# Post-norm weights moved into ScalarE's copy of the output group; the residual scaled and added two chunks at a time

## The reference, cut to what matters

```python
def rms_norm(x, g):
    xf = x.astype(jnp.float32)
    y = xf * lax.rsqrt(jnp.mean(xf * xf, axis=-1, keepdims=True) + EPS)
    return (y * g.astype(jnp.float32)).astype(x.dtype)

def half_ffn(x, g_pre, g_post, w_in, w_out):
    gate, up = jnp.split(rms_norm(x, g_pre) @ w_in, 2, axis=-1)
    return x + 0.5 * rms_norm((jax.nn.silu(gate) * up) @ w_out, g_post)
...
    for i in range(DEPTH):
        xp = half_ffn(xp, g[0], g[1], ffn_w_in[i, 0], ffn_w_out[i, 0])
        ...
        xp = xp + rms_norm(yp, g[3])
        ...
        xp = half_ffn(xp, g[4], g[5], ffn_w_in[i, 1], ffn_w_out[i, 1])
```

## Time and profile before

| | |
|---|---|
| time, median of 3 runs | 2374.84 us (2372.28 to 2375.91) |
| span of the profiled execution | 2375.1 us |
| PE busy | 2213.7 us, 93% of the span |
| DVE busy | 1457.4 us, 61% |
| ACT busy | 941.8 us, 40% |
| POOL busy | 158.0 us, 7% |
| granted TensorE clock, mean | 0.955 of full speed |

### The profile page before, as it was taken

How to read it: one execution, slowest core, us unless ns; L and a number is a source line. 1 busy time by engine, 2 the same in 40 slices (tenths; PEclk the granted TensorE clock), 3 DMA queues, 4 the chain that set the end, 5 groups by cost and what they waited for, 6 DMA issues and landing times.

```text
span 2375.1 us, 41971 instructions
## 1 busy us (share of the span) xinstructions
PE 2213.7 (93%) x17475; PEld 2129.9 (90%) x17475; DVE 1457.4 (61%) x1727; ACT 941.8 (40%) x1111; POOL 158.0 (7%) x214
## 2 busy tenths in 40 slices
PE   7999989999999979899999999779999999998997
PEld 6999989998998945789989998468999999898997
DVE  5665866646655567366656645655664665686663
ACT  3443344444434335244344434324443444433442
POOL 3001010001001000010010001001000000101000
PEclk9999999999999989889999999979999999898998
DMA  6554445553554434245545554414554555354550
GB/s 204 177 196 142 160 144 163 185 201 125 177 195 136 161 113 142 89 142 178 188 131 178 186 188 141 143 45 127 183 189 149 166 185 187 118 178 133 185 188 28
DMA packets 286121, 370.76 MB, mean 156 GB/s; under 512 B 12247, under 2 KB 212360, under 8 KB 285924
## 3 DMA queue, kind: packets, MB, share of 16 engines
q1 hardware_dynamic: 282378, 364.57, 46.0%
q10 hardware_dynamic: 3610, 4.28, 0.5%
HBM read 364.87 MB, written 8.11 MB: 157 GB/s over the span
## 4 chain that ended last, share of the span: by engine, by line
PE 56%; DVE 5%; POOL 1%; issue 1%; ACT 0%; ACTq 0%; DVEq 0%; POOLq 0%
PE ps L1371 15%; PE ps L1373 15%; PE ps L1372 15%; PE ps L1423 1%; PE ps L1424 1%; PE ps L1427 1%; PE ps L1677 1%; POOL rs L609 1%; PE ps L1590 1%; DVE kt_dec L1176 1%; DVE probs L1123 1%; PE ps L1547 1%; PE ps L1580 1%; PE ps L1379 1%; PE ps L1390 1%
## 5 line engine op out<-in xcount | busy, mean ns | idle before, releaser
L1371 PE MATMUL ps<-x_hi,w_high_ring 128*128 128x264 f32 x3112 | 893.8, 287 | 0.0
L860 DVE TENSOR_TENSOR w_low_ring<-wstage,w_high_ring 128x2048 fp32r<-128x2048 f32 x332 | 728.4, 2228 | 262.7 <-ACT w_high_ring L630 184.2
L1373 PE MATMUL ps<-x_hi,w_low_ring 128*128 128x264 f32 x3112 | 889.2, 286 | 0.0
L1372 PE MATMUL ps<-x_lo,w_high_ring 128*128 128x264 f32 x3112 | 888.2, 285 | 0.0
L1372 PEld LDWEIGHTS ps<-x_lo,w_high_ring 128*128 128x128 f32 x3112 | 592.8, 190 | 0.0
L1371 PEld LDWEIGHTS ps<-x_hi,w_high_ring 128*128 128x128 f32 x3112 | 591.3, 190 | 0.8 <-issue 0.2
L1373 PEld LDWEIGHTS ps<-x_hi,w_low_ring 128*128 128x128 f32 x3112 | 591.5, 190 | 0.0
L1371 PE MATMUL ps<-h_hi,w_high_ring 128*128 128x264 f32 x1664 | 474.4, 285 | 4.1 <-issue 4.1
L1373 PE MATMUL ps<-h_hi,w_low_ring 128*128 128x264 f32 x1664 | 474.9, 285 | 0.0
L1372 PE MATMUL ps<-h_lo,w_high_ring 128*128 128x264 f32 x1664 | 473.2, 284 | 0.0
L630 ACT ACTIVATE w_high_ring<-wstage 128x2048 fp32r<-128x2048 f32 (+2 forms) x172 | 307.1, 1816 | 311.6 <-PE ps L1373 299.7
(11 more groups left out here) (287 smaller groups left out, 1898.5 us busy)
## 6 DMA issues: line engine op xcount, KB each, us to landing
wstage<-in_ffn_w_in_dram SPq DMA_DIRECT2D x352, 512.0 KB, 5.0
wstage<-in_ffn_w_out_dram SPq DMA_DIRECT2D x160, 512.0 KB, 4.6
wstage<-in_conv_w_in_dram SPq DMA_DIRECT2D x48, 512.0 KB, 4.9
wstage<-in_nsa_w_in_dram SPq DMA_DIRECT2D x20, 512.0 KB, 4.8
wstage<-in_ffn_w_out_dram SPq DMA_DIRECT2D x32, 256.0 KB, 3.3
wstage<-in_conv_w_out_dram SPq DMA_DIRECT2D x16, 512.0 KB, 4.8
wstage<-in_cache_nsa_dram SPq DMA_DIRECT2D x16, 512.0 KB, 4.6
wstage<-in_diff_w_in_dram SPq DMA_DIRECT2D x16, 512.0 KB, 4.9
```

The lines of the kernel that those rows point to most:

```text
L860: V.tensor_tensor(w_low_ring[:, u % RING, 0:n, 0:cols], wstage[:, stage_of["w", u] % RING, 0:n, 0:cols], w_high_ring[:, u % RING, 0:n, 0:c ...
L1371: MM(out, wh, hi, start=first, stop=False)
L1372: MM(out, wh, lo, start=False, stop=False)
L1373: return MM(out, wl, hi, start=False, stop=last)
```

## The change

ACT's copies of the output to `y` multiply by the post norm's weight of the tile. A weight is one number per partition and per tile, so the copy of the first group, one instruction of 128x1056, becomes four of 128x264. DVE's `scale_y` is then a plain product with `r_post`, over two chunks in one instruction, with `r_post` read twice; the addition to `x` takes two chunks too, and the two `low_x` that follow are those of the pair before. The squares are still taken from PSUM, without the weight.

```diff
-                nc.scalar.activation(y[:, 0:GT, :], gset(g), ACT.Copy).then_inc(y_copied, 1)
+                for tile in range(GT):
+                    ins = nc.scalar.activation(y[:, tile, :], gset(g)[:, tile, :], ACT.Copy, scale=post_gain(s, tile))
+                ins.then_inc(y_copied, 1)
...
-                    nc.scalar.activation(y[:, GT + tile, :], gset(g)[:, tile, :], ACT.Copy)\
+                    nc.scalar.activation(y[:, GT + tile, :], gset(g)[:, tile, :], ACT.Copy, scale=post_gain(s, GT + tile))\
...
                 def scale_y(c):
-                    V.scalar_tensor_tensor(out=y[:, c, :], in0=y[:, c, :], scalar=post_gain(s, c),
-                                           in1=r_post, op0=ALU.mult, op1=ALU.mult).then_inc(y_scaled, 1)
+                    V.tensor_tensor(y[:, c:c + 2, :], y[:, c:c + 2, :], r_post.unsqueeze(1).broadcast_to([P, 2, T]),
+                                    ALU.mult).then_inc(y_scaled, 2)
 
                 scale_y(0)
-                for c in range(NC):
-                    dve.wait_ge(y_scaled, NC * s.i + c + 1)
-                    V.tensor_tensor(x[:, c, :], x[:, c, :], y[:, c, :], ALU.add).then_inc(x_updated, 1)
-                    if c + 1 < NC:
-                        scale_y(c + 1)
+                for c in range(0, NC, 2):
+                    dve.wait_ge(y_scaled, NC * s.i + c + 2)
+                    V.tensor_tensor(x[:, c:c + 2, :], x[:, c:c + 2, :], y[:, c:c + 2, :], ALU.add).then_inc(x_updated, 2)
+                    if c + 2 < NC:
+                        scale_y(c + 2)
                     if c and s.i + 1 < len(subs):
+                        low_x(subs[s.i + 1], c - 2)
                         low_x(subs[s.i + 1], c - 1)
                 if s.i + 1 < len(subs):
                     dve.wait_ge(x_updated, NC * (s.i + 2))
+                    low_x(subs[s.i + 1], NC - 2)
                     low_x(subs[s.i + 1], NC - 1)
```

## The result

The changed kernel takes 2384.77 us in the median of 4 runs (2384.2 to 2386.88), the kernel before 2373.56 beside it (4 runs, 2369.79 to 2375.91). The ratio is 1.005, 95% interval 1.0033 to 1.0066: slower by half a per cent, 8 to 16 us. The forecast of 2382 us and its sign were right; the cost is somewhat larger than forecast. The profiled execution has a span of 2382.4 us (its own time is 2384.4) and a mean granted clock of 0.953.

A forecast was written before the change was run, and what follows sets the result against it. PE, busy 93% of the span, was taken to bound the kernel, with its idle places and lower-clock stretches. Terms +4.6, +0.9, -1.4 and +3.2 add +7.3 us to 2375.1: forecast 2382 us, 8-in-10 range 2375 to 2388.

The forecast's parts named there:

- The restart: At nine sublayer boundaries PE restarts 0.51 us later, as chunk 0 waits for two-chunk scaling and addition: +4.6 us.
- The first `x_lo`: Behind nine restarts, the first low part of x reaches PE's matmuls 0.1 us late, bounds 0 and 0.3: +0.9 us.
- The last sublayer: At the kernel's end, PE's transposes start 5.65 us after the first scaling instead of 7.08: -1.4 us.
- ACT's copies: Copies out of PSUM with the weight, each bounded by 0.39 and 0.50 us: nothing, or 8 us if cover went.
- DVE's saving: Scaling and addition at each boundary take DVE 1.6 us less, which PE does not wait for: worth nothing.
- The clock: PE's time at the lower clock behind restarts and in a later wait, shifted by the delay: +3.2 us, bounds -4 and +8.
- the second dip: Lower clock 13 to 27 us behind a restart, across PE's pre norm wait, plain at three of ten restarts; 2.7 us.
- The sum: Whole kernel: 4.6 + 0.9 - 1.4 + 3.2 = +7.3 us on the profiled 2375.1 us; forecast 2382 us, +0.3%.
- No change: Rival for the whole kernel: clock's part nil, first low part of x just in time, 2378 us; chance 0.33.
- Faster by DVE's saving: Rival: DVE's 1.6 us less at each of twelve boundaries shortens the kernel, 2356 us; chance 0.07 for both faster cases.
- faster by lost dips: Rival: all three later clock dips at PE's pre norm wait go, 2370 us; most of the 0.07 for both faster cases.
- The slow scaling: Rival: scaling with the repeated PSUM operand costs 0.96 us, delaying PE's restart and the first low part, 2389 us; chance 0.06.

The follow-up runs named there:

- The pure delay: Kernel before, plus a spare 128x528 addition (0.63 us) ahead of the first scaling at each boundary: 2384.69 us, ratio 1.0048.
- the kernel with the earliest restart and busy gaps: Changed kernel with the first two chunks scaled and added singly, then pairs, plus 24 spare matmuls per boundary in PE's waits: 2360.12 us, ratio 0.9954.

## Why the prediction was right

**The restart.** Forecast +0.51, measured +0.56, nine times 5.0 us instead of 4.6. The durations were right (0.70 and 0.71). The step that was off is the gap between a scaling and the addition that needs it: I took 0.04 from narrow instructions, and it is 0.10 here, 1228.12 + 0.70 to 1228.92.

**The first `x_lo`.** Forecast 0.1 us late, bounds 0 to 0.3; measured 0.26 by the wait of the weight loads, 2.4 us instead of 0.9. By when PE goes on to the second chunk, 3.10 us behind the restart (1230.33 to 1233.43) instead of 2.78, it is 0.32. Two gaps of 0.10 are part of it; the rest is the `x_lo` itself, two of which take 1.64 us beside POOL's summing, not 0.48 to 0.63 each.

**The last sublayer.** -1.2 instead of -1.4, the same gaps, four of them.

**ACT's copies.** At nothing, and borne out by the kernel that has them alone (0.9991, at most 4 us by the interval). They cost 0.48 us each, inside the bounds of 0.39 and 0.50.

**DVE's saving.** At nothing: the kernel that keeps the later pairs and not the first is no faster (0.9987). The price was right, its reason was not: there is no saving, and the sign is the other way. I took 0.71 for all additions; at 0.96 the eight chunks cost 4 x (0.70 + 0.96) = 6.6 us, not 5.7, against 7.3 before, `x_lo` takes 0.07 longer, eight times, and the overlaps of 0.08 between instructions are fewer. The prediction had the last `x_hi` of a boundary 1 us earlier. It starts 10.21 us behind the first scaling instead of 9.25, here before and then changed:

```profile
1236.61 0.52 ACT L645 ACTIVATE x_hi<-x,gains 128x264 fp32r<-128x264 f32 x1 [0.43 <-DVE x L1351]
```

```profile
1238.33 0.50 ACT L645 ACTIVATE x_hi<-x,gains 128x264 fp32r<-128x264 f32 x1
```

PE does not wait for it in either kernel, so the error cost the forecast nothing.

The Trainium skill, page "VectorE: DVE Perf Modes", in its section on the TRN2 errata, recommends wide tiles to spread the fixed latency. Here the advice costs 5 us of restarts before the clock has a say, since the first result of the row is what PE waits for.

**The clock.** The sign was right, the size not: +3.2, of which I spoke mainly as a later return behind the restart. That part is 2.3 us. The larger one is the second dip, which I had named, with a price for one dip more at the upper bound only: five plain dips instead of three and two half ones instead of one, 8.4 us by the two profiles. (It counted three among ten restarts; there are eleven. Its upper bound of +8 comes to 7.2 by its own terms.) By the mean clocks of the runs the two parts together are some 6 to 8 us: 224 us at the lower level in the changed kernel, 202 to 206 in the kernel before in the other batches, and some 7 of the difference are PE's longer waits. The pure delay shows that it is the lateness that costs this, not the instructions: 6.2 us of delay make 12.3, still 11.7 with the restart's spell removed, and 0.6 us a sublayer once the second wait is filled. That the second dip follows a long low spell at the restart is what the stages show; why, and why the kernel with the earliest restart and busy gaps has the most dips, is open. No run here moves the wait by itself.

**The sum** of +7.3 on 2375.1 stands against +11.2 by the medians, just below the interval of 8 to 16. That 2382 lies within 3 us of 2384.77 is in part luck: 1.5 us come from the base, since the kernel before took 2373.56 beside the changed one. The terms that were too small are the clock (3.2 for 6 to 8) and the first `x_lo` (0.9 for 2.4).

**The rivals.** No change fell, by the interval. Faster by DVE's saving fell with the two kernels above; faster by lost dips went the other way. The slow scaling fell, at 0.70; the late `x_lo` that it was to bring came in part all the same, from the additions' gaps and POOL.

## What to carry to other kernels

Where the next engine waits for the first result of a series, keep the first instructions narrow and widen only what lies behind them, if at all: with TensorE at full clock the pairs behind the first two chunks still cost half a microsecond a sublayer. A saving per instruction is worth nothing until it is on the path, and the sum of durations is not the time that a series takes. A delay of half a microsecond ahead of a TensorE restart can cost twice its length through the clock in the next wait, so look at the granted clock by stage, in the waits behind the restart too, before judging an order. If such dips are there, filling those waits with work that exists, or with spare matmuls, is worth more than the order: 2.2% here, against the 0.5% that was at stake.

## What had not been expected

An addition of 128x528 with both inputs in SBUF takes 0.71 us alone and 1.25 when an instruction of POOL's summing has begun just before it (22 of 48); the scaling of the same width, with one input in PSUM, takes 0.69 in both places. The Trainium skill, page "SBUF — State Buffer", section "Who interferes with whom", says that a VectorE instruction with two SBUF inputs contends with a GpSimd instruction that reads SBUF, and one with a single SBUF input (outside the two-port modes) does not. The trace agrees in both. It shows too that the order of the two matters: in the kernel before 64 of the 96 additions of 128x264 run beside POOL's summing, and the 62 that began first take 0.42 to 0.43 us, as alone, the two that began behind it 0.97 and 0.98. With pairs, all 22 that run beside it begin behind it.

Twenty-four spare matmuls a sublayer, put where PE only waits, make the kernel 0.87% faster (0.9913). And PE at full clock makes the change dearer: its wait for `x_lo` rises from 0.26 to 1.06 us a boundary, because PE is ready sooner.
